# Moving small block transfers from ScalarE's queue to GpSimd's, and cutting one substitution into five pieces

## The reference

```python
L = jnp.where(strict, jnp.einsum('nbhcd,nbhsd->nbhcs', k_beta, kb) * decay, 0.0)
eye = jnp.eye(C, dtype=L.dtype)
tinv = lax.linalg.triangular_solve(eye + L, jnp.broadcast_to(eye, L.shape),
                                   left_side=True, lower=True, unit_diagonal=True)
```

## Time and profile before

| | |
|---|---|
| median of 3 executions | 2079.91 us (2075.92 to 2086.56) |
| profiled execution, its own time | 2088.29 us |
| its span, first to last instruction | 2086.6 us |
| mean granted TensorE clock | 0.955 |
| mixing turns, layer 0 and layer 1 | about 280 to 765 us and 1310 to 1785 us |
| transfers of the block steps | 108, all from ScalarE: 48 gather, 6 fetch, 6 store, 48 scatter |

### The profile page before, as it was taken

How to read it: one execution, slowest core, us unless ns; L and a number is a source line. 1 busy time by engine, 2 the same in 40 slices (tenths; PEclk the granted TensorE clock), 3 DMA queues, 4 the chain that set the end, 5 groups by cost and what they waited for, 6 DMA issues and landing times.

```text
span 2086.6 us, 45340 instructions
## 1 busy us (share of the span) xinstructions
PE 1923.2 (92%) x19380; PEld 1749.4 (84%) x19380; DVE 1254.1 (60%) x2158; ACT 938.9 (45%) x1834; POOL 4.8 (0%) x30
## 2 busy tenths in 40 slices
PE   6999989889999898899999999988899998789998
PEld 4899978778888787788989998888799788679997
DVE  3555356656445567677656654566654565859963
ACT  3334464344456523433444444644443754253343
POOL 0000000000000000000000000000000000000000
PEclk8999999999999989999999999998899998899999
DMA  7877754565454564699756666453443435359973
GB/s 251 240 230 212 210 167 144 151 173 158 129 166 136 144 157 113 189 282 271 197 167 172 182 178 186 142 147 107 127 131 98 135 97 132 82 147 254 260 198 112
DMA packets 580070, 353.37 MB, mean 169 GB/s; under 512 B 44004, under 2 KB 539654, under 8 KB 578318
## 3 DMA queue, kind: packets, MB, share of 16 engines
q1 hardware_dynamic: 490634, 302.74, 50.8%
q10 hardware_dynamic: 89236, 47.74, 9.2%
HBM read 332.27 MB, written 18.50 MB: 168 GB/s over the span
## 4 chain that ended last, share of the span: by engine, by line
PE 70%; DVE 12%; DMA 7%; ACT 5%; issue 3%; ACTq 2%; SPq 0%; DVEq 0%
PE bank L898 68%; DMA ring<-in_ffn_up 2%; DVE ring_r L740 2%; DMA ring<-in_w_ada 2%; DVE far L1964 2%; ACT w_hi_r L732 1%; DVE big L1964 1%; PE bank L653 1%; DMA far<-in_state_gdn_ssm 1%; ACTq L634 1%; PE bank L666 1%; DMA far<-t_blocks 1%; DVE far L1967 1%; DVE big L615 1%; DVE big L614 1%
## 5 line engine op out<-in xcount | busy, mean ns | idle before, releaser
L898 PE MATMUL bank<-big_r,w_hi_r 128*128 128x264 f32 x4160 | 1077.5, 293 | 46.3 <-DVE h_r L1967 25.2
L898 PE MATMUL bank<-big_r,ring_r 128*128 128x264 f32 (+1 forms) x3456 | 995.1, 288 | 0.0
L898 PEld LDWEIGHTS bank<-big_r,w_hi_r 128*128 128x128 f32 x4160 | 749.9, 192 | 108.6 <-issue 88.0
L898 PE MATMUL bank<-h_r,w_hi_r 128*128 128x264 f32 x2752 | 798.0, 290 | 0.0
L740 DVE TENSOR_TENSOR ring_r<-ring,w_hi_r 128x1024 fp32r<-128x1024 f32 (+2 forms) x440 | 523.6, 1195 | 424.9 <-ACT w_hi_r L732 421.4
L898 PEld LDWEIGHTS bank<-big_r,ring_r 128*128 128x128 f32 (+1 forms) x3456 | 663.7, 192 | 1.0
L732 ACT CAST w_hi_r<-ring 128x1024 fp32r<-128x1024 f32 (+2 forms) x440 | 452.0, 1028 | 454.8 <-PE bank L898 207.2
L898 PEld LDWEIGHTS bank<-h_r,w_hi_r 128*128 128x128 f32 x2752 | 531.4, 193 | 1.7 <-issue 0.5
L898 PE MATMUL bank<-big,far 64*64 64x64 f32 (+2 forms) x1440 | 110.0, 266 | 0.0
L898 PE MATMUL bank<-ring,c 128*32 128x256 f32 x1152 | 95.3, 412 | 13.1 <-DMA ring<-in_w_ada 10.1
L898 PEld LDWEIGHTS bank<-big,far 64*64 64x64 f32 (+1 forms) x1440 | 92.1, 147 | 8.1 <-issue 7.5
(11 more groups left out here) (297 smaller groups left out, 1893.0 us busy)
## 6 DMA issues: line engine op xcount, KB each, us to landing
ring<-in_ffn_up SPq DMA_DIRECT2D x176, 512.0 KB, 4.9
ring<-in_w_in SPq DMA_DIRECT2D x148, 512.0 KB, 3.7
ring<-in_w_ada SPq DMA_DIRECT2D x144, 512.0 KB, 3.9
ring<-in_ffn_down SPq DMA_DIRECT2D x64, 512.0 KB, 4.3
far<-in_state_gdn_ssm ACTq DMA_DIRECT2D x28, 512.0 KB, 5.8
ring<-in_ffn_down SPq DMA_DIRECT2D x32, 384.0 KB, 3.5
ring<-in_w_out SPq DMA_DIRECT2D x16, 512.0 KB, 4.4
out_sample_gdn_ssm<-far ACTq DMA_DIRECT2D x16, 512.0 KB, 4.9
```

Of the source, the lines that this page charges most:

```text
L898: return pe.matmul(out, lhsT, rhs, start=start, stop=stop)
```

## The change

Every transfer of `gather`, `fetch`, `store` and `scatter`, for all three lots, is issued by GpSimd, in one block per layer that stands ahead of the turn loops. GpSimd has no turns: it goes down the list gather, fetch, store, scatter of run 0, then of run 1, then of run 2, with the same waits as before. ScalarE keeps `clear`. The substitution of run 0 moves from turns 20 and 21 to turns 21, 23, 24, 26 and 27, and stands behind `prep` in each of them; runs 1 and 2 keep their turns, their halves and their place.

```diff
-GATHER0, FETCH0, SOLVE0, STORE0 = (18, 30, 66), (19, 31, 67), (20, 32, 68), (22, 34, 69)
-CLEAR0, SCATTER0, INV0 = (29, 35, 67), (30, 36, 70), (32, 38, 72)
+CLEAR0, INV0 = (29, 35, 67), (32, 38, 72)
+SOLVE = ({21: (1, 4), 23: (4, 7), 24: (7, 10), 26: (10, 12), 27: (12, 15)}, {32: (1, 7), 33: (7, 15)}, {68: (1, 7), 69: (7, 15)})
...
-                act.dma_start(lt_blocks[part_of, :, :].rearrange("u s t -> s u t"), lt[rows, :, cols]).then_inc(block_in.sem, block_in.one())
+                pool.dma_start(lt_blocks[part_of, :, :].rearrange("u s t -> s u t"), lt[rows, :, cols]).then_inc(block_in.sem, block_in.one())
...
-            if half == 0:
+            if first == 1:
...
-            for s in (range(1, 7) if half == 0 else range(7, B16 - 1)):
+            for s in range(first, min(end, B16 - 1)):
...
-            if half == 1:
+            if end == B16 - 1:
...
+                @block.gpsimd
+                def _(pool):
+                    for run in range(3):
+                        gather(pool, run)
+                        fetch(pool, run)
+                        store(pool, run)
+                        scatter(pool, run)
...
-                            if t == GATHER0[run] and run < 2:
-                                gather(act, run)
-                            if t == FETCH0[run]:
-                                fetch(act, run)
-                            if t == STORE0[run] and run < 2:
-                                store(act, run)
-                            if t == SCATTER0[run]:
-                                scatter(act, run)
...
-                        if t == GATHER0[2]:
-                            gather(act, 2)
-                        if t == STORE0[2]:
-                            store(act, 2)
...
-                            if 0 <= t - SOLVE0[run] < 2:
-                                solve(dve, run, t - SOLVE0[run])
+                            if run and t in SOLVE[run]:
+                                solve(dve, run, *SOLVE[run][t])
...
                         for j in range(NT):
                             prep(j, t - PREP0 - 3 * j)
+                        if t in SOLVE[0]:
+                            solve(dve, 0, *SOLVE[0][t])
```

More of the change, by code:

```diff
@@ L567, in square, with gather, fetch, store @@
             return buf.rearrange("p (a b) -> p a b", a=B16)
-        def gather(act, run):
+        def gather(pool, run):
             lt = inv_sets[run][0]
             if run == 2:
-                act.wait_ge(gdn_dve.sem, gdn_dve.at(H_B - 1))
+                pool.wait_ge(gdn_dve.sem, gdn_dve.at(H_B - 1))
             else:
-                act.wait_ge(prod_dve.sem, prod_dve.at(4 * run + 4))
+                pool.wait_ge(prod_dve.sem, prod_dve.at(4 * run + 4))
             if run:
-                act.wait_ge(block_in.sem, block_in.at(9 * run))
+                pool.wait_ge(block_in.sem, block_in.at(9 * run))
             for rows, cols, part_of in blocks():
-                act.dma_start(lt_blocks[part_of, :, :].rearrange("u s t -> s u t"), lt[rows, :, cols]).then_inc(block_in.sem, block_in.one())
-        def fetch(act, run):
-            act.wait_ge(block_in.sem, block_in.at(9 * run + 8))
+                pool.dma_start(lt_blocks[part_of, :, :].rearrange("u s t -> s u t"), lt[rows, :, cols]).then_inc(block_in.sem, block_in.one())
+        def fetch(pool, run):
+            pool.wait_ge(block_in.sem, block_in.at(9 * run + 8))
             if run:
[L585 to L590, removed]
+                pool.wait_ge(solved.sem, solved.at(run))
+            pool.dma_start(square(solve_bufs[run][0]), lt_blocks[:, :, :]).then_inc(block_in.sem, block_in.one())
+        def store(pool, run):
+            pool.wait_ge(solved.sem, solved.at(run + 1))
             if run:
-                act.wait_ge(block_out.sem, block_out.at(9 * run))
-            act.dma_start(t_blocks[:, :, :, :], solve_bufs[run][1]).then_inc(block_out.sem, block_out.one())
-        def solve(dve, run, half):
+                pool.wait_ge(block_out.sem, block_out.at(9 * run))
+            pool.dma_start(t_blocks[:, :, :, :], solve_bufs[run][1]).then_inc(block_out.sem, block_out.one())
+        def solve(dve, run, first, end):
             got, both, prod = solve_bufs[run]
@@ L626, in clear, with scatter @@
             i.then_inc(inv_z.sem, inv_z.one())
-        def scatter(act, run):
-            act.wait_ge(inv_z.sem, inv_z.at(run + 1))
-            act.wait_ge(block_out.sem, block_out.at(9 * run + 1))
+        def scatter(pool, run):
+            pool.wait_ge(inv_z.sem, inv_z.at(run + 1))
+            pool.wait_ge(block_out.sem, block_out.at(9 * run + 1))
             into = inv_sets[run][1].rearrange("p u t w -> p u (t w)")
             for rows, cols, part_of in blocks():
-                act.dma_start(into[rows, :, 2 * cols.start:2 * cols.stop], t_blocks[part_of].rearrange("u s t w -> s u (t w)")).then_inc(block_out.sem, block_out.one())
+                pool.dma_start(into[rows, :, 2 * cols.start:2 * cols.stop], t_blocks[part_of].rearrange("u s t w -> s u (t w)")).then_inc(block_out.sem, block_out.one())
         def invert(pe, run, s):
@@ L2331, in _ @@
                             dve.memset(e65[:, :, 0:1], 1.0).then_inc(e_one.sem, e_one.one())
-                        if t == STORE0[1] + 3:
+                        if t == 37:
                             dve.wait_ge(block_out.sem, block_out.at(18))
```

## The result

| | before | after |
|---|---|---|
| median | 2077.91 us (2075.20 to 2086.56, 4 executions) | 2047.20 us (2038.88 to 2055.65, 4 executions) |
| ratio, 95% interval | | 0.9835 (0.9806 to 0.9863) |
| profiled execution, own time | 2088.29 us | 2038.88 us |
| mean granted TensorE clock | 0.955 | 0.971 |

The change made the kernel 31 us faster, where 12 us slower had been forecast. It is the first rival, GpSimd issuing fast, that came. The ratio given is not the quotient of the two medians, which is 0.9852.

What follows compares the result with a forecast made beforehand. TensorE, busy 92% of the span, was taken to bound the kernel. The terms, -16 + 2(17x - 10.0) + 2(8x - 4.9) + 2(18x - 19.1), gave +12.3 us at x = 1.12: 2092 us from 2079.9, range 2055 to 2132.

Steps and rivals of the forecast that it cites:

- the first rival: GpSimd issues fast enough: below x = 0.86 the kernel is faster, 2049 us at x = 0.47; chance 0.33.
- The unknown x: Time GpSimd takes to issue one transfer, put at 1.12 us, the middle between 0.47 and 1.76.
- -84 + 86x: Sum of the four terms in us against the kernel before; +12.3 us at x = 1.12.
- term 4: Run 2: gather to substitution 9x - 10.1, store to product 9x + 7.5 against 16.5; +2.1 us in two layers.
- Term 1: Run 0's gather and substitution: TensorE's long periods between turns 17 and 29 return to about 15.7 us; -16 us.
- The rival that the pieces don't fit: Above x = 1.16 turn 21's piece waits for the fetch, at x = 1.76 by 5.4 us a layer.
- Term 2: Turn 32, runs 0 and 1 meet: run 1's substitution starts 17x - 10.0 = 9.0 us late; +18.1 us in two layers.
- Term 3: Turn 38: run 1's scatter lands after its product's old start, 8x - 4.9 = 4.1 us; +8.1 us in two layers.
- the prediction's sign: Profile sign for run 2: in turn 68 the substitution's operation L608 is released by the fetch.
- VectorE holds GpSimd up: Rival: GpSimd prepares transfers only while VectorE is idle, x = 2.0, sum +88, 2168 us; chance 0.03.
- Landing times: Kept for GpSimd's transfers: 3.5 us for a gather, 2.4 fetch, 3.5 store, 4.0 scatter.

Runs made afterwards that it cites:

- run 0: Not a follow-up kernel: the first of the three lots of block transfers (gather, fetch, store, scatter) in each layer, with its substitution; no time of its own.
- the queue alone: GpSimd issues all transfers, run 0's substitution stays in two halves ahead of `prep` in turns 20 and 21, against the kernel before: 2062.03 us, ratio 0.9879.
- the pieces alone: ScalarE issues as before, run 0's store at turn 28, its substitution in five pieces behind `prep`, against the kernel before: 2082.66 us, ratio 0.9979.
- x = 2.12: The changed kernel with five memsets on GpSimd, each waited for, ahead of every transfer: 2190.09 us, ratio 1.0491 to the kernel before.
- one memset: The changed kernel with one waited-for memset on GpSimd ahead of every transfer, x = 1.07: 2103.79 us, ratio 1.0084 to the kernel before.
- two memsets: The changed kernel with two waited-for memsets on GpSimd ahead of every transfer, x = 1.34: 2113.72 us, ratio 1.0135 to the kernel before.
- the second profile: A second profile of the unaltered changed kernel, taken later: own time 2059.52 us.

## Why the prediction was wrong

The unknown x is the step that failed, and the only one that turned the sign: "Neither end is nearer, so I take the middle, x = 1.12 us". It was 0.56. The sum around it, -84 + 86x, came within about 10 us at four values of x. What waits for what was right where the transfers are slow (x of 1.07 and more); at x = 0.56 one of its paths, the first half of term 4, was not the one that the trace shows.

The middle of the two bounds was a poor choice between them. The upper one, 1.76 us, was a single issue out of 48 while the median was 0.47; a row nearer to the question stood in the text itself, the seven issues in a row at 4.63/7 = 0.66 us. It was used for the rival, where it gave -27 us, and the result is -31. ScalarE's other rows give 0.49 to 0.67 us each. What a row of issues costs should have been read from a row of issues.

- **Term 1** (-16 predicted, -19.9 and -19.3 measured). Its cause is shown: the queue alone removes the 5.37 us gap, the pieces alone don't, and both together leave gaps of 0.56 to 1.36 us and no half clock. The 1 us a layer for pieces that stick out was not needed. The rival that the pieces don't fit shows only at x = 2.12, where turn 23's product waited 4.73 us and the term fell to -7.5. The condition given for it, x above 1.16, was too early: at 1.34 there is no loss yet. The prediction let the gather start 376.07 - 367.92 = 8.15 us after turn 17's product, as ScalarE did; GpSimd started it 370.73 - 365.09 = 5.64 us after. By the prediction's own working that moves the condition to x above 1.44, an estimate from these rows.
- **Term 2** (+18.1 predicted). At x = 0.56, 17x - 10.0 is -0.5 us, and VectorE's first operation of run 1's substitution came 453.19 - 429.56 = 23.63 us after turn 29's product, against 24.37 before: -0.7. One thing was left out. That ScalarE is free of 16 issues in turn 30 was priced at nothing; before, they held 6.84 and then 1.56 us of ScalarE's time, and with the pieces alone 6.81 and 2.81. With the substitution on time this may be worth something, but no run separates it from the rest of the term.
- **Term 3** (+8.1). 8x - 4.9 is -0.4 at 0.56: the wait ahead of run 1's first product was 0.83 us in the one profile and 1.39 in the other, against 1.23. With one memset it was 2.46 us in layer 0 and with two 4.62, where the term gives 1.2 + 3.7 = 4.9 and 1.2 + 5.8 = 7.0: it was priced too high there.
- **Term 4** (+2.1; 36x - 38.2 = -18.0 at 0.56). Measured -17.4 and -11.1. Run 2's first product now follows a wait of 0.65 us (2.70 in the second profile). The rival had allowed 10 us for both layers. That the term's number fits so well is in part luck. Its second half holds: from the store to the product it took 701.71 - 689.86 = 11.85 us, 4.6 less than before, where 9x + 7.5 - 16.5 says 4.0. Its first half does not: from the first issue of the gather to the substitution it took 679.16 - 666.20 = 12.96 us, 3.0 less than the 695.70 - 679.73 = 15.97 before, where 9x - 10.1 says 5.1 less. The fetch did not release the substitution, as the prediction's sign had it; VectorE came to it without idle time, behind a low part that had waited for ScalarE's cast. Only with the memsets does the fetch end VectorE's wait here (2.55 us with one).
- **VectorE holds GpSimd up.** It fell. During the eight issues of the scatter, 438.28 to 442.76, VectorE was busy 3.74 of 4.48 us, and the issues took 4.48; during those of the gather from 370.73 on it was busy 2.32 of 4.58. In the 16 us around the latter it was busy 10.33. The Trainium skill ("SBUF — State Buffer", Who interferes with whom) warns of it for copies and tensor-scalar operations in their two-port modes. In the changed kernel's profile no copy ran during any of the 108 issues, and a tensor-scalar operation only met the first 20 ns of a gather, so the trace agrees with the page but does not test that case.

```profile
363.00:379.00 16.00, 15.36 (x179) 13.52 (x178) 10.33 (x20) 7.28 (x18) 4.58 (x8) 1.00 0.69 202
```

- **Landing times.** They were kept, and they stayed. The Trainium skill ("DMA: Bandwidth & Descriptors", Specifications) gives GpSimd's path a longer time to the first byte. No row shows the first byte; the medians from issue to landing, 3.2 and 4.1 us for the eights, against 3.5 and 4.0, show no such difference. They don't compare like with like: the page of the profile counts 27840 packets less on ScalarE's queue (89236 and 61396) and 3840 on GpSimd's, for the same 4.73 MB. Whether fewer packets are a part of the gain was not tested; the weights landed as before (4.9 and 4.8 us for those of `ring<-in_ffn_up`, 3.7 and 3.7 for `ring<-in_w_in`).

What stays open is the row "rest". It is time outside the stretches that the change touches, and in the changed kernel's two profiles it is -9.5 and +3.5, the spread between executions. With the memsets it is 8 to 13 us of loss in all three, and the clock may be a part of that. In the 60 us from run 2's first product on, in layers 0 and 1, the granted clock was 0.89 and 0.91 before and 0.83 and 0.81 with one memset:

```profile
724.80:784.80 60.00, 57.65 (x772) 50.72 (x773) 32.97 (x36) 16.33 (x29) 0.00 (x0) 0.83 0.56 142
1749.80:1809.80 60.00, 56.68 (x749) 50.37 (x750) 32.15 (x35) 17.26 (x30) 0.00 (x0) 0.81 0.49 121
```

Over 60 us that is 0.06 x 60 + 0.10 x 60 = 9.6 us, an estimate from these clocks, against 9.1 measured. With two memsets it is 0.82 and 0.85, so 7.8 of 13.1. But the changed kernel's second profile also has 0.86 and 0.91 there, with a wait of 2.70 us at the same product, so no run shows how much of the clock belongs to the longer wait and how much to the single execution.

## What to carry to other kernels

Transfers that a busy engine issues in a row cost that engine the whole row, and whatever stands behind them in its order; here moving them to an idle queue that is no faster for each was worth 24 of 2086 us, and ScalarE's wait for the landed eight went with them. Price a row of issues by a row of issues, not by the median or the longest single one; and where one unknown carries the whole sum, the formula in it is the forecast, and its middle is not evidence. An edit that shortens one wait is worth only what the next one leaves: look at the engine that is released sooner, and at what stands behind its next piece of work.

## What the runs showed of the hardware

- An issue on GpSimd took 562 to 689 ns, median 564, whether the transfer was 16, 32, 128 or 256 KB, and whether VectorE was busy or not. ScalarE's, for 16 KB, took 309 to 1759 ns, median 470. In the kernel before its rows of seven took 3.44 to 4.63 us and its rows of eight 3.97 to 5.36.
- TensorE's clock was lower in one stretch where it waited more. With one memset TensorE waited 9.4 us at three places of layer 0 between 445 and 496 us, and from 450 to 520 its mean granted clock was 0.83, against 0.98 before. In the changed kernel the waits there were 4.4 us and the clock 0.96.

```profile
450.00:520.00 70.00, 62.35 (x920) 56.62 (x920) 36.38 (x78) 24.26 (x53) 13.48 (x35) 0.83 0.47 125
```

- A memset of 128 by 128 on GpSimd with its wait added 0.51 us as the first ahead of a transfer, of which 0.22 is the memset and 0.29 lies between its end and the transfer's start. Each further one added 0.26 us.
- The profile counts 3840 packets for the 108 transfers from GpSimd's queue, where ScalarE's queue had 27840 for the same 4.73 MB.
